# One modulation vector moved from the start of the expert stage into the first mixer

## The reference, cut to what matters

```python
for l in range(DEPTH):                                   # DEPTH = 2
    m = jax.nn.silu(c) @ mod_w[l] + mod_b[l]             # 1024 -> 6 * 1024
    sh1, sc1, g1, sh2, sc2, g2 = jnp.split(m[:, None, :], N_MOD, axis=-1)
    h = rms_norm(x, norm1_g[l]) * (1.0 + sc1) + sh1
    y = attn_gmlp_mixer(h, ...) if l == 0 else multiscale_pool(h, ...)
    x = x + g1 * y
    h2 = rms_norm(x, norm2_g[l]) * (1.0 + sc2) + sh2
    x = x + g2 * peer_ffn(h2, ...)
```

## Time and profile before

| | us |
|---|---|
| median of 3 runs | 2671.64 |
| lowest and highest of them | 2666.89, 2674.22 |
| the profiled execution, its own time | 2669.8 |
| span of the profiled execution, first to last instruction | 2667.9 |
| busy in the span: TensorE products, VectorE, ScalarE, GpSimd | 2367.8, 1850.8, 1219.5, 645.7 |

### The profile page before, as it was taken

One profiled execution on the slowest core, in us unless ns is written; L12 is line 12 of the kernel. 1 busy time (PEld: TensorE's weight loads), 2 busy tenths in 40 slices (PEclk: granted clock), 3 DMA queues, 4 the chain that ended last, 5 costly groups with the idle time before them and its releaser, 6 DMA issues. The chain is left out here.

```text
span 2667.9 us, 35241 instructions
## 1 busy us (share of the span) xinstructions
PE 2367.8 (89%) x12935; PEld 1577.4 (59%) x12936; DVE 1850.8 (69%) x3447; ACT 1219.5 (46%) x2595; POOL 645.7 (24%) x547
## 2 busy tenths in 40 slices
PE   6988788888888989888888899999999998978999
PEld 4774333333334444343332278898888887866887
DVE  4777776678667867867775566676666666797665
ACT  3433434444445544444434354456445444445543
POOL 0003445553444444455554300000000000003000
PEclk9998999999999999999999999999999999979999
DMA  9799999999999999999999965542555554213553
GB/s 383 283 386 415 403 427 427 426 427 422 425 412 420 374 426 406 426 427 427 427 423 427 427 232 188 188 158 95 183 183 186 185 184 177 105 50 118 185 187 112
DMA packets 121705, 811.26 MB, mean 304 GB/s; under 512 B 15713, under 2 KB 18825, under 8 KB 26584
## 3 DMA queue, kind: packets, MB, share of 16 engines
q0 software_dynamic: 74160, 540.05, 48.4%
q1 hardware_dynamic: 47400, 269.32, 28.1%
HBM read 807.12 MB, written 1.15 MB: 303 GB/s over the span
## 5 line engine op out<-in xcount | busy, mean ns | idle before, releaser
L1487 PE MATMUL bank<-rows,diag 128*128 128x512 f32 (+1 forms) x2060 | 990.9, 618 | 201.9 <-ACT diag L1659 201.0
L1905 DVE CUSTOM_DVE_ANT_0 rows<-rows,h 128x1024 f32<-128x1024 f32 (+1 forms) x512 | 620.0, 1224 | 354.2 <-DMA rows<-in_peer_rows,idx 348.2
L1487 PEld LDWEIGHTS bank<-rows,diag 128*128 128x128 f32 (+1 forms) x2060 | 371.4, 194 | 724.5 <-ACT diag L1659 404.0
L1340 POOL DMA_INDIRECT rows<-in_peer_rows,idx x512 | 610.3, 1192 | 726.5 <-PE bank L1487 668.3
L1650 ACT ACTIVATE picks<-picks 128x1 f32<-128x1 f32 (+1 forms) x512 | 103.3, 202 | 623.8 <-DVE picks L1905 616.8
L2246 PE MATMUL bank<-hT_pair,halves 128*128 128x512 f32 x864 | 307.4, 399 | 0.4 <-DVE hT_pair L2124 0.4
L2247 PE MATMUL bank<-hT_pair,halves 128*128 128x256 f32 x864 | 242.3, 280 | 0.0
L1659 ACT ACTIVATE diag<-const_table,picks 128x128 f32<-128x128 f32 (+1 forms) x512 | 205.5, 401 | 48.0 <-ACT picks L1654 1.1
L2180 DVE TENSOR_TENSOR halves<-weight_ring,halves 128x2048 fp32r<-128x2048 f32 x73 | 166.9, 2288 | 72.2 <-ACT halves L2175 72.1
L2246 PEld LDWEIGHTS bank<-hT_pair,halves 128*128 128x128 f32 x864 | 162.3, 188 | 41.3 <-DVE hT_pair L2124 0.9
L1372 PE MATMUL bank<-halves_b,halves_a 128*128 128x256 f32 x864 | 165.8, 334 | 0.0
(11 more groups left out here) (600 smaller groups left out, 3776.4 us busy)
## 6 DMA issues: line engine op xcount, KB each, us to landing
weight_ring<-in_ffn_w_gate SPq DMA_DIRECT2D x44, 1024.0 KB, 4.9
weight_ring<-in_ffn_w_up SPq DMA_DIRECT2D x44, 1024.0 KB, 4.8
weight_ring<-in_ffn_w_down SPq DMA_DIRECT2D x44, 1024.0 KB, 4.8
mod_ring<-in_mod_w SPq DMA_DIRECT2D x16, 1024.0 KB, 9.8
weight_ring<-in_peer_w_q SPq DMA_DIRECT2D x16, 1024.0 KB, 10.7
half_ring<-in_mod_w SPq DMA_DIRECT2D x24, 512.0 KB, 7.5
rows<-in_mod_w SPq DMA_DIRECT2D x12, 1024.0 KB, 10.6
weight_ring<-in_attn_w_in SPq DMA_DIRECT2D x12, 1024.0 KB, 4.9
```

The costliest lines, as they stand in the source:

```text
L1340: nc.gpsimd.indirect_dma_start(ring[:, s], None, dram["peer_rows"], bass.IndirectOffsetOnAxis(ap=idx[:, T, n:n + 1], axis=0)).then_inc(row ...
L1487: mm = nc.tensor.matmul(bank[:, :], diag[0:n, j % DIAG_SLOTS], ring[0:n, j % ROW_SLOTS, D + half * 512:D + (half + 1) * 512], start=(j in ...
L1905: dotted.up(nc.vector.tensor_tensor_reduce(out=ring[r, s, 0:D], in0=ring[r, s, 0:D], in1=its_h, scale=1.0, scalar=0.0, op0=ALU.mult, op1=A ...
```

## The change

The vector (1, 3) goes from `LATE` to `MULTIPLIED`, as its fifth. Its four chunks pass through `mod_ring` in the mixer. TensorE multiplies 20 chunks there instead of 16: two instead of one after each of `project(4)`, `project(5)` and `project(6)`, and one more after unit 6. Eight late chunks are left, one for each slot of `rows`, so none of them reuses a slot. SP's list is rearranged: `fetch(sp, 2)` stands ahead of the store of (0, 3), halves stand ahead of the next two chunks, and so on as shown. The additions of the second and third vector move in VectorE's list. The bias lines in `mod_line` grow from 3 to 4.

```diff
-    MULTIPLIED = [(0, 2), (0, 4), (1, 1), (1, 0)]
+    MULTIPLIED = [(0, 2), (0, 4), (1, 1), (1, 0), (1, 3)]
     SUMMED = [(0, 3), (0, 5), (1, 2)]
-    LATE = [(1, 3), (1, 4), (1, 5)]
+    LATE = [(1, 4), (1, 5)]
@@ SP's list in first_block
                 rows.store(sp, (0, 2))
                 rows.fetch(sp, 2)
                 rows.fetch_halves(sp, 2)
+                rows.fetch(sp, 2)
                 rows.store(sp, (0, 3))
                 rows.fetch_halves(sp, 1)
-                rows.fetch(sp, 1)
                 rows.fetch_halves(sp, 2)
-                rows.fetch(sp, 1)
+                rows.fetch(sp, 2)
                 rows.fetch_halves(sp, 2)
                 sp.wait_ge(masked.sem, m0 + len(units))
                 sp.wait_ge(rows.stored.sem, rows.stored_at((0, 2)))
                 gate_in.up(sp.dma_start(g1, rows.row(0, 2)), 16)
                 rows.store(sp, (0, 4))
-                rows.fetch(sp, 1)
                 rows.fetch_halves(sp, 3)
+                rows.fetch(sp, 2)
                 rows.store(sp, (0, 5))
                 rows.fetch(sp, 1)
                 rows.fetch_halves(sp, 3)
+                rows.fetch(sp, 1)
                 sp.wait_ge(mixed.sem, mi0 + HEADS)
@@ TensorE's list
                 project(4, {(0, 2): 0, (0, 6): 2, (1, 3): 4}).then_inc(W.multiplied, 1)
-                rows.multiply(pe, 1)
+                rows.multiply(pe, 2)
                 project(5, {(0, 2): 6, (0, 6): 8, (1, 3): 10}).then_inc(W.multiplied, 1)
-                rows.multiply(pe, 1)
+                rows.multiply(pe, 2)
                 project(6, {(0, 1): 12, (0, 5): 14}).then_inc(W.multiplied, 1)
-                rows.multiply(pe, 1)
+                rows.multiply(pe, 2)
                 rows.reduce(pe, 1)
...
-                    if j in (3, 9, 12):
+                    if j in (3, 6, 9, 12):
                         rows.multiply(pe, 1)
@@ VectorE's list
                 rows.accumulate(dve, 2)
+                rows.add(dve, 4)
                 rows.add_sum(dve, 0)
...
                 rows.accumulate(dve, 1)
-                rows.add(dve, 4)
                 mask(14)
                 mask(15)
                 shift(1)
                 rows.accumulate(dve, 3)
+                rows.add(dve, 4)
                 for j in range(HEADS):
@@ buffers: mod_line [P, 3, BLK] becomes [P, 4, BLK], and the bias columns are split 4:8 and 8:10 instead of 4:7 and 7:10
```

More of the change, by code:

```diff
@@ L4062, in build @@
                 with kit.sb("mod_ring", [P, MOD_SLOTS, KD * BLK]) as ring, kit.sb("half_ring", [P, HALF_SLOTS, D]) as half_ring, \
-                        kit.sb("mod_line", [P, 3, BLK]) as line:
+                        kit.sb("mod_line", [P, 4, BLK]) as line:
                     early = vec[:, 0, :].rearrange("p (s n) -> p s n", n=BLK)
                     sums = kit.hT[:].rearrange("p k n -> p (k n)").rearrange("p (a n) -> p a n", a=2)
-                    rows.place(ring, half_ring, sums, [early[:, v] for v in range(4)] + [line[:, v] for v in range(3)], cwide)
+                    rows.place(ring, half_ring, sums, [early[:, v] for v in range(4)] + [line[:, v] for v in range(4)], cwide)
                     first_block(kit, dram, rows, vec, [(early[0:P:32, :, :], early[:], bias[:, 0:4]),
-                                                       (line[0:P:32, :, :], line[:], bias[:, 4:7])], shared, kit.first_root)
-                experts(kit, dram, rows, vec, bias[:, 7:10], shared, kit.first_root)
+                                                       (line[0:P:32, :, :], line[:], bias[:, 4:8])], shared, kit.first_root)
+                experts(kit, dram, rows, vec, bias[:, 8:10], shared, kit.first_root)
         second = contextlib.ExitStack()
```

## The result

The changed kernel takes 2679.07 us (median of 20 executions, 2671.97 to 2685.78) against 2670.7 us (20 executions, 2666.89 to 2684.68) for the kernel before: ratio 1.0029, 95% interval 1.002 to 1.0038, which is 5 to 10 us slower. The forecast was 2671.0 us in a range up to 2679. Run again it gave 2681.28 against 2673.66 us, ratio 1.0023 (1.001 to 1.0036).

What follows compares the result with a forecast made beforehand. It took the expert stage as bound by DMA and the mixer by TensorE. Mixer +6.0 us and expert stage -6.6 us net -0.6 us: 2669.2 us by the profiled execution, 2671.0 us as median, range 2664 to 2679.

Steps and rivals of the forecast that it cites:

- the term for new waits in the mixer: TensorE before unit 3: chunk 12, asked for late, makes it wait 0, 2.4 or 7.1 us; taken as 1.3 us.
- the 0.4 us for the first copy: Mixer: halves 16 and 17 land later, delaying VectorE's first copy of turned probabilities; 0.4 us more wait (0 to 2.0).
- +6.0 us for the mixer: Mixer's whole added cost: 3.8 matmuls, 0.5 store, 0.4 first copy, 1.3 wait for chunk 12.
- asked for 4 us later, like their use: Mixer: output weights are requested 4 us later, as they are used later; costed at nothing.
- The 3.8 us for the matmuls: Mixer: four added chunks on TensorE, three at 0.93 us and one at 1.0, uncovered; bounds 3.6 and 4.0.
- The third store: Mixer's end: one more store for SP costs 0.51 us, taken as 0.5; 0 if only the issue counts.
- forecast 6.6 (5.8 to 7.1): Expert stage: four late chunks removed save 9.8 us, less 3.2 us of grown DMA hole.
- The hole before the first gather: Start of expert stage: DMA engines idle until gather bytes flow; the 1.2 us loss grows by 3.2 us (2.7 to 4.0).
- The two rules: Skill's first byte at about 1 us would give 2669.8 us; its ring order for chunk 12, 2669.7 us; neither was followed.
- A chunk comes late: Rival, TensorE before unit 3: wait of 7.1 instead of 1.3 us, total 2676.8 us; chance 0.15.
- The gain stops at the routing work: Rival, expert stage: VectorE's picks make gathers run dry; half of the 6.6 us lost, 2674.3 us; chance 0.11.
- the mixer took nothing in: Rival, mixer: TensorE's idle time absorbs 3 us of the 6.0 added, total 2668 us; chance 0.14.

Runs made afterwards that it cites:

- after_again: The changed kernel run again unaltered, for a second profiled execution; 2681.28 us against 2673.66 us for the kernel before, ratio 1.0023.
- cost_only: Changed kernel with vector (1, 3) made twice, in the mixer and late in the expert stage; 2681.72 us, ratio 1.004 to the kernel before.
- stem_after: Changed kernel cut off behind the first block's expert stage; by the medians 7 us more than the kernel before cut off there.
- mix_after: Changed kernel cut off behind the first block's mixer, x written out there; 197.3 us against 187.3 us for the kernel before cut alike.
- mix_first: Changed kernel cut off behind the mixer, with only halves 16 and 17 asked for earlier, in turn with chunks 10 and 11; 198.49 us.
- mix_second: Changed kernel cut off behind the mixer, with only chunks 12 and 13 asked for behind half 18 instead of half 20; 197.19 us.
- after_ordered: Changed kernel with SP's order mended: halves 16, 17 in turn with chunks 10, 11, and chunks 12, 13, 15 earlier; 2675.98 us, ratio 1.001 to the kernel before.
- mix_mended: Changed kernel cut off behind the mixer: halves 16, 17 accumulated between probability copies, chunks 12 to 15 asked for earlier, ScalarE's rounding behind its last copy; 194.05 us.
- mended_after: Whole changed kernel with both mixer holes mended, half 20 accumulated later, half 23 asked for behind chunks 16 and 17; 2671.02 us, ratio 0.9995 to the kernel before.
- the cut mixers: The kernel before and the changed kernel, each cut off behind the first block's mixer; 187.3 and 197.3 us.
- after_kept: Changed kernel with 16 filler matmuls of 256 columns on TensorE while it waits for chunk 12; 2685.66 us, ratio 1.0058 to the kernel before.
- gain_only: Kernel before without vector (1, 3): four fewer late chunks, none added to the mixer, row (1, 0) read instead; 2667.05 us, ratio 0.9985.
- pause_short: Kernel before with VectorE filling a dead buffer three times in 512 columns after the expert stage, a 2.0 us pause; 2672.0 us, ratio 0.9995.
- pause_long: Kernel before with three VectorE fills of 1024 columns after the expert stage, a 3.6 us pause; 2679.44 us, ratio 1.0021.
- clock_before: Kernel before with filler matmuls on TensorE in the second block, before the recurrence; 2672.59 us, ratio 1.0007.
- stem_before: Kernel before cut off behind the first block's expert stage; by the medians 7 us less than the changed kernel cut off there.
- mended_before: Whole kernel before with the same edits of VectorE, ScalarE and SyncE's halves as the mended changed kernel; 2670.64 us, ratio 0.9991.
- the cuts: Both kernels cut off behind the mixer and behind the expert stage; by the medians the change costs 10 us in the mixer, 7 us in the first block.

## Why the prediction was wrong

**The step that failed** is the term for new waits in the mixer: chunk 12, "a wait of 0, 2.4 or 7.1 us", taken as 1.3 us, with "Behind this wait stand all later units", and the 0.4 us for the first copy. Together they allow 1.7 us of new idle time. Both waits were found in the right place by the right reasoning, and both were sized too small. In the first profile TensorE's four holes sum to 5.71 us, against 2.06 us in the two holes of the kernel before (1.06 and 1.00), counted behind 85 us: 3.65 us more, and that profile has the cheapest mixer of the unmended ones. Before chunk 12 the wait is 1.99, 2.82 and 3.52 us in three profiles, before the first value product 1.3 to 1.8 us. What the runs show in place of +6.0 us for the mixer is +7.8 us where the clock was kept (below) and 10 to 11 us by the times.

**The clock.** The prediction has no term for TensorE's clock in the mixer, and in some executions the waits are followed by a stretch of value products at half clock. By windows of 1 us it amounts to 13.7 us at half clock in `after_again`, 10.2 in `cost_only`, 13.6 in `stem_after`, 6.8 in `mix_after`, and 3.4 each in `mix_first` and `mix_second`; half of that, 1.7 to 6.9 us, is lost on the engine that sets the mixer's end. In `cost_only` and `stem_after` TensorE doesn't wait for chunk 12 at all, because its clock has been at half since 124 and 122 us, behind the first hole. Among the profiled mixers with five vectors the clock fell at 120 to 140 us in six of the eight that had one or both holes, and in none of the three with both mended (`after_ordered`, `mix_mended`, `mended_after`). With four vectors it fell there in none of nine. The first gather starts at 208.0 to 208.9 us in the four whole kernels with five vectors that kept the clock there, mended or not, and at 212.6 to 217.0 in the three where it fell.

So in single executions the loss is plain. That it is what the change costs on average is not shown. The profiled executions are one of each run, and over all executions the mean granted clock is the same: 0.933 and 0.937 in the cut mixers, and 0.9715 (103 executions of the kernel before) against 0.9724 (20 of the changed one) in the whole kernels, which tells less, since bytes set the pace of the expert stage. The run that was to keep the clock with the wait in place, `after_kept`, got slower. How the cost beyond 6.0 us divides into idle time and clock stays open.

A shorter fall, 3.4 us at half clock and so 1.7 us lost, comes later, between 143 and 162 us, in nine of the twenty profiles, and the kernel before is one of them. Its timeline and its window:

```profile
143.77 0.98 PE L787 MATMUL bank<-proj,vectors 128*128 128x64 f32 x4 [1.00 <-ACT vectors L918]
```

```profile
140.00:150.00 10.00, 9.00 (x71) 8.49 (x61) 8.21 (x19) 4.24 (x6) 0.00 (x0) 0.83 1.00 404
```

It stands behind a hole of 1.00 us there. The sign was in the trace that the prediction was built on.

**The mixer's other terms.** Five vectors and no fall cost more than 6.0 us too. The first gather is issued at 208.65 and 208.85 us in the two unmended mixers that kept the clock, and at 200.9 us in the mean over the seven kernels with four vectors in the mixer (table below, `gain_only` among them and not `cost_only`): +7.8 us. The profile that the prediction was built on, 203.09, is the latest of those seven, its own fall of the clock being part of that; the +5.6 us of the first pair is flattered by it. Beyond 6.0 stand the larger waits above, 0.43 us at chunk 15, 1.46 us at the last copy against 1.0, and the wait for the output weights: "asked for 4 us later, like their use" was costed at nothing, and ScalarE rounds them at 147.91 instead of 141.33 us, 6.6 us later. The 3.8 us for the matmuls is borne out by the rows (1.07 us for a group of 16, as before). The third store took 1.54 us with its two fellows instead of 1.02, as costed.

**The expert stage.** By the profiles it is confirmed, by the times only within their scatter. From the issue of the first gather to the last addition of x it took 1341.7 to 1346.3 us, mean 1344.0, in seven profiles with three late vectors, and 1336.3 to 1339.0 us, mean 1337.8, in seven with two: a gain of **6.2 us**, forecast 6.6 (5.8 to 7.1). By profile, start of the first gather on GpSimd, start of the last addition on VectorE, and the time between, in us:

```
three late vectors                        two late vectors
before         203.09  1545.32  1342.2    after          208.65  1546.94  1338.3
pause_short    201.54  1546.63  1345.1    after_again    216.96  1555.77  1338.8
pause_long     200.60  1542.33  1341.7    after_ordered  208.41  1544.68  1336.3
clock_before   202.08  1548.41  1346.3    after_kept     208.85  1547.85  1339.0
stem_before    198.52  1543.78  1345.3    gain_only      200.21  1536.65  1336.4
mended_before  200.37  1545.05  1344.7    stem_after     212.57  1551.32  1338.8
cost_only      213.55  1555.92  1342.4    mended_after   208.00  1544.95  1337.0
```

The hole before the first gather costs (1 - 55/427) + 3 + (1 - 115/427) + (1 - 262/427) = 5.0 us of DMA time where it cost 1.2, so it grew by 3.8 us, forecast 3.2 (2.7 to 4.0). By the times alone the gain is smaller, 4.0 us in `gain_only` and 3 us between the cuts, both with at least some 2.5 us of uncertainty; whether that is scatter stays open. So of the 8.3 us between forecast (-0.6) and measurement (+7.7), `cost_only` puts 4.7 into the mixer and `gain_only` 2.6 into the gain, and only the first is clear of its interval.

**The two rules.** The Trainium skill (DMA: Bandwidth & Descriptors, Latency and other measured facts) with its first byte at about 1 us for a transfer that GpSimd issues would have put bytes at 209.7; the first window that has any is 211 to 212, at least 2.3 us after the issue, so the row was the better guide. The comparison in the prediction was uneven, though: the Trainium skill's figure is for the first byte, the row's 2.2 us for the full rate. From the Trainium skill (the same page, Queues, rings and completion order) the prediction had worked out a wait for chunk 12 nearer 0; in the four profiles in which TensorE waits for it in full the traces show 1.9 to 3.5 us.

**The rivals.** "A chunk comes late" named the place and even the point of decision (slower from a wait of 1.9 us, a landing 7.5 us after the issue; measured 1.99 and 7.5 in the first profile) and got 0.15, and it too priced idle time only. "The gain stops at the routing work" isn't needed, and the mixer took nothing in.

**Checked by the mended kernel.** Mixer +7.6 us (first gather at 208.00 against 200.37 in `mended_before`), expert stage 1336.95 against 1344.68 us, -7.7: net 0 in this pair, and +0.4 us in the medians. The trade that the prediction described exists; the kernel as changed doesn't make it.

## What to carry to other kernels

Where TensorE sets the end of a stage, add up every hole that a new order of transfers opens, not only the one asked for late, and allow for a stretch at half clock behind it. Here the holes grew by 3.65 us where 1.7 was allowed, and holes of 1.3 to 3.5 us were followed by another 1.7 to 6.9 us lost at half clock in six of eight profiles. Before calling the clock the cause, compare its mean over all executions: here it was no lower after than before. Two holes close together had to be mended together here before the median moved. A transfer that is asked for later "like its use" can still land late: look up who waits for it. When the effect is smaller than the scatter of one execution, compare the same stretch over many profiles, or cut the program behind the stage and time that: a single pair of profiles put 6.5 of 8 us into a block that had no part in it.

## What was not expected of the hardware

The clock is a matter of the execution: the same changed kernel kept 1.00 in one profile at 130 to 150 us and was at 0.53 and 0.79 in the next. So is the recurrence's: around its first steps (2394 to 2423 us) it was at half clock for 3.4 us in six of twelve profiles, 6.8 in three, and 10.2, 13.7 and 20.5 in one each, with either mixer. In `after_kept`, whose second block is one of the long ones, they have 3.4 us, so the length isn't set there alone. And filler matmuls in a wait are no sure cure. With 16 of them before chunk 12 the hole shrank from 1.99 to 0.39 us and the kernel got slower, 2685.66 us, for a reason that no run here shows.
